# Five weight slots in place of four for the FFN input units of a decoder layer, with loads reordered and one subtraction split in time

## The reference, cut to what matters

```python
def swiglu_ffn(x, w_in, w_out):
    gate, up = jnp.split(x @ w_in, 2, axis=-1)
    return (jax.nn.silu(gate) * up) @ w_out
...
x = x + 0.5 * swiglu_ffn(rmsnorm(x, ffn1_norm[l]), ffn1_w_in[l], ffn1_w_out[l])
...
x = x + 0.5 * swiglu_ffn(rmsnorm(x, ffn2_norm[l]), ffn2_w_in[l], ffn2_w_out[l])
```

## Time and profile before

| | us |
|---|---|
| median of 3 runs | 1762.08 (1761.79 to 1765.37) |
| profiled execution, its own time | 1763.39 |
| span of the profiled execution, first to last instruction | 1761.5 |

### The profile page before, as it was taken

The page is one execution under the profiler, slowest core; times in us unless marked ns, Lnnn a source line. Parts: engine busy times, 40 slices in busy tenths (PEclk is TensorE's granted clock), DMA queues, the critical chain, the costliest instruction groups (busy, mean ns, idle before and its releaser), DMA issues.

```text
span 1761.5 us, 21397 instructions
## 1 busy us (share of the span) xinstructions
PE 1749.1 (99%) x7976; PEld 1448.9 (82%) x7976; DVE 1483.3 (84%) x1778; ACT 1108.7 (63%) x1461; POOL 95.1 (5%) x111
## 2 busy tenths in 40 slices
PE   9999999999999999999999999999999999999999
PEld 7888888888888888888888888888888888987887
DVE  7999989998999998575655655988999999899998
ACT  7666666666666666454545554666666666666665
POOL 0000010000000001100000000100000000000000
PEclk9999999999999999999999999999999999999999
DMA  9898888886655556555455457888888897764762
GB/s 378 285 287 270 263 257 262 259 254 193 248 215 193 202 214 209 189 181 185 155 186 168 168 168 269 268 261 262 265 272 273 266 278 213 241 214 165 256 214 92
DMA packets 168326, 405.02 MB, mean 230 GB/s; under 512 B 9016, under 2 KB 18000, under 8 KB 162848
## 3 DMA queue, kind: packets, MB, share of 16 engines
q1 hardware_dynamic: 154208, 342.03, 54.0%
q0 software_dynamic: 12896, 59.67, 16.7%
q10 hardware_dynamic: 1120, 1.97, 0.3%
HBM read 351.57 MB, written 5.79 MB: 203 GB/s over the span
## 4 chain that ended last, share of the span: by engine, by line
PE 94%; DVE 3%; ACT 1%; issue 1%; DMA 0%; SPq 0%; DVEq 0%; ACTq 0%
PE bank L697 8%; PE bank L669 8%; PE bank L671 8%; PE bank L670 8%; PE bank L699 8%; PE bank L698 8%; PE bank L630 7%; PE bank L632 7%; PE bank L631 6%; PE bank L777 5%; PE bank L779 5%; PE bank L778 5%; PE bank L803 3%; PE bank L805 3%; PE bank L804 3%; DVE wlo L1332 2%
## 5 line engine op out<-in xcount | busy, mean ns | idle before, releaser
L1332 DVE TENSOR_TENSOR wlo<-raw,whi 128x1024 fp32r<-128x1024 f32 (+1 forms) x506 | 609.2, 1209 | 199.1 <-ACT whi L973 187.4
L973 ACT ACTIVATE whi<-raw 128x1024 fp32r<-128x1024 f32 (+1 forms) x506 | 527.8, 1048 | 356.0 <-PE bank L632 183.8
L697 PE MATMUL bank<-whi,xs 128*128 128x512 f32 (+1 forms) x608 | 239.3, 394 | 6.4 <-DVE wlo L1332 5.5
L699 PE MATMUL bank<-whi,xs 128*128 128x512 f32 (+1 forms) x608 | 234.7, 386 | 0.0
L698 PE MATMUL bank<-wlo,xs 128*128 128x512 f32 (+1 forms) x608 | 234.3, 385 | 0.0
L973 ACT ACTIVATE whi<-tsum 128x1024 fp32r<-128x1024 f32 (+1 forms) x120 | 122.2, 1037 | 98.6 <-PE bank L699 47.0
L777 PE MATMUL bank<-whi,aw_hi 128*128 128x512 f32 x420 | 164.4, 391 | 0.0
L779 PE MATMUL bank<-whi,aw_lo 128*128 128x512 f32 x420 | 163.6, 389 | 0.0
L778 PE MATMUL bank<-wlo,aw_hi 128*128 128x512 f32 x420 | 163.5, 389 | 0.0
L630 PE MATMUL bank<-whi,xs 128*128 128x512 f32 x384 | 155.1, 404 | 0.4 <-DVE wlo L1332 0.4
L1332 DVE TENSOR_TENSOR wlo<-tsum,whi 128x1024 fp32r<-128x1024 f32 (+1 forms) x120 | 141.7, 1194 | 12.4 <-ACT whi L973 10.7
(11 more groups left out here) (225 smaller groups left out, 3092.4 us busy)
## 6 DMA issues: line engine op xcount, KB each, us to landing
raw<-ffn_w_in SPq DMA_DIRECT2D x86, 1024.0 KB, 7.0
raw<-ffn_w_out SPq DMA_DIRECT2D x84, 1024.0 KB, 6.7
raw<-w_in SPq DMA_DIRECT2D x48, 1024.0 KB, 5.0
raw<-ffn_w_in SPq DMA_DIRECT2D x75, 512.0 KB, 7.6
tsum<-raw POOLq DMA_DIRECT2D x35, 1024.0 KB, 7.0
minis<-ffn_w_in SPq DMA_DIRECT2D x72, 256.0 KB, 8.0
last_plain<-ffn_w_in SPq DMA_DIRECT2D x36, 512.0 KB, 6.0
raw<-w_out SPq DMA_DIRECT2D x16, 1024.0 KB, 4.9
```

The costliest lines, as they stand in the source:

```text
L697: mm(banks[b][:, 0:w], xs[:, k + i, 0, tok], hi, start=starts[b] and k + i == 0, stop=False, skip_group_check=True)
L699: last = mm(banks[b][:, 0:w], xs[:, k + i, 1, tok], hi, start=False, stop=k + i == last_k, skip_group_check=True)
L973: A(whi[:, h % SLOTS, 0:n_el], src, ACT.Copy).then_inc(weights_hi, 1)
L1332: V.tensor_tensor(wlo[:, h % SLOTS, 0:n_el], src, whi[:, h % SLOTS, 0:n_el].bitcast(f32), ALU.subtract).then_inc(weights_lo, 1)
```

## The change

Four things, all in the units of both FFNs:

1. In units 1 to 9 the halves go through a ring of five slots. The fifth, `fifth`, lies in slot 1 of `raw`. Slots in these units are counted from the first half of unit 1, modulo five; before and after them a half's slot is h % 4 as it was. ACT waits for the half that had the slot last, whichever it was (`RING_LAST`). At unit 1 ACT also waits until all of unit 0 has been split, since `fifth` lies where one of its pieces was.
2. Each of the four form pieces has one slot of `raw` and of `minis` of its own (2, 3, 4, 0) in place of five in turn.
3. SP's order in a unit j is B11 of the next unit; UA, UB, UC; B12, B22, B21 of the next unit; GA, GB, GC of the next unit. It was B12 of the next unit; UA, UB; B22; UC; B21; B11 of the unit after the next; GA, GB, GC.
4. The gate's first combination adds bank X first, between B22's two halves on DVE, and subtracts bank Y afterwards, ahead of T4; it was first Y ahead of T4, then X between T4's two halves. PE waits ahead of UA for the subtraction, as before.

```diff
-FORM_SLOTS, FIRST_FORM_SLOT = 5, 2
+FORM_RAW = (2, 3, 4, 0)
+FIFTH_RAW = 1
+FIRST_OUT_SLOT = 2
...
+def ring_slot(h):
+    for u in range(2):
+        if unit_half(u, 1) <= h < unit_half(u, UNITS - 1):
+            return (h - unit_half(u, 1)) % (SLOTS + 1)
+    return h % SLOTS
+
+RING_LAST, _seen = {}, {}
+for _h in range(END):
+    RING_LAST[_h] = _seen.get(ring_slot(_h), -1)
+    _seen[ring_slot(_h)] = _h
...
-            return (4 * j + i + FIRST_FORM_SLOT) % FORM_SLOTS if i < 4 else RAW_SLOTS + (i - 4) % 3
+            return FORM_RAW[i] if i < 4 else RAW_SLOTS + (i - 4) % 3
...
+        place[0] = raw_at + FIFTH_RAW * 4 * W * 4
+        fifth = sb("fifth", [P, 2, 2 * W], f32r)
...
+        def hi_of(h):
+            return whi[:, ring_slot(h), :] if ring_slot(h) < SLOTS else fifth[:, 0, :]
...
+                if slot == FIFTH_RAW:
+                    for u in range(2):
+                        if OUT_P[u] <= n < (QKV_P, END_P)[u]:
+                            sp.wait_ge(weights_used, unit_half(u, UNITS - 1))
...
                         plain_piece(u, 1, "GC")
-                        form_piece(u, 2, "B11")
                     else:
                         if j + 1 < UNITS:
-                            form_piece(u, j + 1, "B12")
-                        plain_piece(u, j, "UA")
-                        plain_piece(u, j, "UB")
+                            form_piece(u, j + 1, "B11")
+                        for name in ("UA", "UB", "UC"):
+                            plain_piece(u, j, name)
                         if j + 1 < UNITS:
-                            form_piece(u, j + 1, "B22")
-                        plain_piece(u, j, "UC")
-                        if j + 1 < UNITS:
-                            form_piece(u, j + 1, "B21")
-                            if j + 2 < UNITS:
-                                form_piece(u, j + 2, "B11")
-                            plain_piece(u, j + 1, "GA")
-                            plain_piece(u, j + 1, "GB")
-                            plain_piece(u, j + 1, "GC")
+                            for name in ("B12", "B22", "B21"):
+                                form_piece(u, j + 1, name)
+                            for name in ("GA", "GB", "GC"):
+                                plain_piece(u, j + 1, name)
...
-                pe.wait_ge(w_done, first + 1)
+                pe.wait_ge(gate_added, 2 * first + 1)
...
             def split(h, src, n_el):
-                if h >= SLOTS:
-                    act_e.wait_ge(weights_used, h - SLOTS + 1)
-                A(whi[:, h % SLOTS, 0:n_el], src, ACT.Copy).then_inc(weights_hi, 1)
+                if RING_LAST[h] >= 0:
+                    act_e.wait_ge(weights_used, RING_LAST[h] + 1)
+                A(hi_of(h)[:, 0:n_el], src, ACT.Copy).then_inc(weights_hi, 1)
...
+                if j == 1:
+                    act_e.wait_ge(weights_lo, base)
...
-                for i in range(2):
-                    split(base + B22 + i, form_half(n22, i, w), w2)
+                split(base + B22, form_half(n22, 0, w), w2)
+                dve.wait_ge(weights_used, base + GC + 1)
+                dve.wait_ge(copied, 3 * first + 1)
+                V.tensor_tensor(gset[:, s, 1, 0:w], X[:, 0:w], gset[:, s, 1, 0:w], ALU.add).then_inc(x_added, 1)
+                split(base + B22 + 1, form_half(n22, 1, w), w2)
                 plain_split("UA", UA)
                 dve.wait_ge(weights_used, base + T3_B22 + 1)
-                dve.wait_ge(copied, 3 * first + 1)
-                V.tensor_tensor(gset[:, s, 1, 0:w], gset[:, s, 1, 0:w], Y[:, 0:w], ALU.subtract).then_inc(w_done, 1)
+                dve.wait_ge(x_added, first + 1)
+                V.tensor_tensor(gset[:, s, 1, 0:w], gset[:, s, 1, 0:w], Y[:, 0:w], ALU.subtract).then_inc(gate_added, 1)
                 split(base + T4, t_half(0, w), w2)
-                dve.wait_ge(w_done, first + 1)
-                V.tensor_tensor(gset[:, s, 1, 0:w], X[:, 0:w], gset[:, s, 1, 0:w], ALU.add).then_inc(gate_added, 1)
                 split(base + T4 + 1, t_half(1, w), w2)
```

More of the change, by code:

```diff
@@ L148, in raw_slot @@
             q = OUT_LOADS[c][i] - 2 * OUT_GROUPS[c]
-            return 3 + (2 * c * OUT_GROUPS[0] + OUT_LOADS[c][i]) % 3 if q < 0 else (c * ACT_PLAIN[0] + q + FIRST_FORM_SLOT) % 3
+            return 3 + (2 * c * OUT_GROUPS[0] + OUT_LOADS[c][i]) % 3 if q < 0 else (c * ACT_PLAIN[0] + q + FIRST_OUT_SLOT) % 3
     for first, slots in ((IN_P[1], RAW_SLOTS), (QKV_P, QKV_RAW_SLOTS), (0, RAW_SLOTS)):
         if n >= first:
-            return (n - first + (sum(ACT_PLAIN) + FIRST_FORM_SLOT if slots == QKV_RAW_SLOTS else 0)) % slots
+            return (n - first + (sum(ACT_PLAIN) + FIRST_OUT_SLOT if slots == QKV_RAW_SLOTS else 0)) % slots
 def transfers(n):
@@ L304, in piece_half, with lo_of @@
             return raw[:, raw_slot(n), i * n_el:(i + 1) * n_el]
+        def hi_of(h):
+            return whi[:, ring_slot(h), :] if ring_slot(h) < SLOTS else fifth[:, 0, :]
+        def lo_of(h):
+            return wlo[:, ring_slot(h), :] if ring_slot(h) < SLOTS else fifth[:, 1, :]
         def plain_half(n, n_el):
@@ L374, in layer @@
         x_stored, x_back = sem("x_stored"), sem("x_back")
-        sums_done, t2_added, t4_added, t_summed, copied, w_done, gate_added, c11_done = (
-            sem(n) for n in ("sums_done", "t2_added", "t4_added", "t_summed", "copied", "w_done", "gate_added", "c11_done"))
+        sums_done, t2_added, t4_added, t_summed, copied, x_added, gate_added, c11_done = (
+            sem(n) for n in ("sums_done", "t2_added", "t4_added", "t_summed", "copied", "x_added", "gate_added", "c11_done"))
         sq_done, hss_ready, hms_ready, hr_ready, hsc_ready, qn_ready, qk_psum, qkT_ready, v_ready = (
@@ L573, in add_piece @@
                 pool.dma_start(tsum[:, 0:4 * w], raw[:, raw_slot(n), 0:4 * w], accum_op=ALU.add).then_inc(done, 16)
-                pool.dma_start(tmini[:, 0:w], minis[:, raw_slot(n), 0:w], accum_op=ALU.add).then_inc(done, 16)
+                pool.dma_start(tmini[:, 0:w], minis[:, FORM_RAW.index(raw_slot(n)), 0:w], accum_op=ALU.add).then_inc(done, 16)
             def x_again(u):
@@ L666, in tile @@
             def tile(h, i, bank_out, stationary, k, w, start, stop):
-                hi, lo = whi[:, h % SLOTS, i * w:(i + 1) * w], wlo[:, h % SLOTS, i * w:(i + 1) * w]
+                hi, lo = hi_of(h)[:, i * w:(i + 1) * w], lo_of(h)[:, i * w:(i + 1) * w]
                 st_hi, st_lo = stationary(k, 0), stationary(k, 1)
@@ L693, in plain @@
                         pe.wait_ge(x_ready, 2 * h + i + 1)
-                    hi, lo = whi[:, slot, i * w:(i + 1) * w], wlo[:, slot, i * w:(i + 1) * w]
+                    hi, lo = hi_of(h)[:, i * w:(i + 1) * w], lo_of(h)[:, i * w:(i + 1) * w]
                     for b in range(TB):
@@ L970, in split @@
             def split(h, src, n_el):
-                if h >= SLOTS:
-                    act_e.wait_ge(weights_used, h - SLOTS + 1)
-                A(whi[:, h % SLOTS, 0:n_el], src, ACT.Copy).then_inc(weights_hi, 1)
+                if RING_LAST[h] >= 0:
+                    act_e.wait_ge(weights_used, RING_LAST[h] + 1)
+                A(hi_of(h)[:, 0:n_el], src, ACT.Copy).then_inc(weights_hi, 1)
             def split_two(h, src0, src1, w):
-                act_e.wait_ge(weights_used, h - SLOTS + 1)
-                A(whi[:, h % SLOTS, 0:w], src0, ACT.Copy)
-                A(whi[:, h % SLOTS, w:2 * w], src1, ACT.Copy).then_inc(weights_hi, 1)
+                act_e.wait_ge(weights_used, RING_LAST[h] + 1)
+                A(hi_of(h)[:, 0:w], src0, ACT.Copy)
+                A(hi_of(h)[:, w:2 * w], src1, ACT.Copy).then_inc(weights_hi, 1)
             def mixer_split(t):
@@ L1331, in split @@
                 dve.wait_ge(weights_hi, h + 1)
-                V.tensor_tensor(wlo[:, h % SLOTS, 0:n_el], src, whi[:, h % SLOTS, 0:n_el].bitcast(f32),
+                V.tensor_tensor(lo_of(h)[:, 0:n_el], src, hi_of(h)[:, 0:n_el].bitcast(f32),
                                 ALU.subtract).then_inc(weights_lo, 1)
@@ L1336, in split_two @@
                 dve.wait_ge(weights_hi, h + 1)
-                V.tensor_tensor(wlo[:, h % SLOTS, 0:w], src0, whi[:, h % SLOTS, 0:w].bitcast(f32), ALU.subtract)
-                V.tensor_tensor(wlo[:, h % SLOTS, w:2 * w], src1, whi[:, h % SLOTS, w:2 * w].bitcast(f32),
+                V.tensor_tensor(lo_of(h)[:, 0:w], src0, hi_of(h)[:, 0:w].bitcast(f32), ALU.subtract)
+                V.tensor_tensor(lo_of(h)[:, w:2 * w], src1, hi_of(h)[:, w:2 * w].bitcast(f32),
                                 ALU.subtract).then_inc(weights_lo, 1)
```

15 lines of the change are left out of this document (7 added, 8 removed).

## The result

The changed kernel is slower: 1765.62 us (median, 1764.24 to 1767.88) against 1762.14 (1761.57 to 1765.37), a ratio of 1.0018, 95% interval [1.0012, 1.0024]. The prediction, 1757.6 us, is 8 us too low, and the result lies above its range: 3.5 us more in place of 4.5 less. The profiled execution has a span of 1764.6 us against 1761.5.

A forecast was written before the change was run, and what follows sets the result against it. PE (TensorE), busy 99% of the span, was taken to bound the kernel, so only its waiting could change. Terms -9.4 - 0.3 + 5.25 = -4.5 us, off the median 1762.08, gave 1757.6 us; range 1755.2 to 1762.3.

The forecast's parts named there:

- Ring of five, GA: Units 2 to 9 of both FFNs: PE's wait at GA goes, 0.59 us per unit, -9.4 us (-7.7 to -10.2).
- the loads: Reordered loads and a slot per form piece, in both FFNs: 0, up to 1 us per FFN in the upper bound.
- X's place: X added between B22's halves, ahead of PE's UA: nothing queues behind a wait, 0, covered by 1.5 us.
- The borders: Unit 10 of FFN 1 +2.5, unit 10 of FFN 2 +0.85, unit 1 of FFN 2 +1.9; together +5.25 us (4.5 to 6).
- B12's move: B12's load goes out when T3_B22 is split and lands before `sum_t1` needs it, with 1.8 us of cover.
- late-B12 rival: B12 shares the engines with other transfers, `sum_t1` waits in every unit; 1770 us at a 10.5 us landing; chance 0.07.
- Unit 1 of FFN 1: The fifth slot closes a 0.2 us gap between B11's halves; with hitches at the unit's end -0.3 us (0 to -0.5).
- the sentence on W_out: Before FFN-out: W_out's second load waits for B21's slot; 0, up to 1 us for each FFN in the upper bound.
- The clock: Rival: after PE's waits at three borders the clock falls to 1.2 GHz, giving back the 4.5 us; 1762 us; chance 0.04.
- unmoved GA: Rival: SwiGLU waits for something other than DVE's queue, GA's 0.48 us stay; +5, 1767 us; chance 0.05.

The follow-up runs named there:

- e5: Changed kernel with the ring of four halves of before, the new loads, slots and X's place kept; 1770.95 us, ratio 1.0048 against the kernel before.
- e7: Changed kernel with the addition of X put back behind T4's first half; 1767.33 us, ratio 1.0029 against the kernel before.
- e3: Changed kernel with the edits of e1 and e2 together; 1753.60 us, ratio 0.9949 against the kernel before.
- e2: Changed kernel with the ring of five renumbered so that halves at its borders take the slot free longest; 1760.44 us, ratio 0.9986 against the kernel before.
- e1: Changed kernel with W_out's first five transfers in slots 1, 2, 3, 4, 0 instead of 2, 0, 3, 4, 1; 1759.08 us, ratio 0.9979.
- e6: Changed kernel with POOL's 2 MB transfer of x started ten halves later; 1761.39 us, ratio 0.9994 against the kernel before.
- e8: e3 with UC's transfer issued behind B12 of unit 2, in unit 1 alone; 1752.20 us, ratio 0.9942 against the kernel before.
- e9: Changed kernel with the edits of e8 and e6 together; 1754.73 us, ratio 0.9958 against the kernel before.

## Why the prediction was wrong

**Ring of five, GA: right, the total in part by luck.** -9.7 measured for -9.4. Units 2 to 9 are at 41.03 each, and PE waits nowhere in them. But e5 gives 0.09 of a unit's gain to the loads or X's place, which were put at 0: the ring itself is worth 16 x 0.52 = 8.3 us, inside the bounds of its term, and the other 1.4 was not foreseen.

**The borders: right.** 2.61, 0.97 and 1.85 measured, together 5.43, for 2.5, 0.85 and 1.9; the waits stand at T1 (2.08) and GA (0.99), as described, and renumbering the ring took 5.2 us away. The upper bound of the sum, added up from its terms, is +0.3 and not 0; the result lies outside either.

**B12's move: right.** In unit 4 of FFN 1 it left at 200.45, its `minis` part landed at 206.91 and `sum_t1` read it at 208.62: 1.7 us of cover for 1.8. The late-B12 rival did not come. The landing of 6.1 us after the issue of that part is near the row of its new place, and not near 10.3, the longest landing, by which the rival was priced; POOL's sum beside it is over at 203.38. The Trainium skill ("DMA: Bandwidth & Descriptors", section "Queues, rings and completion order") has each DMA engine take turns between the queues that have work. Where a transfer of POOL runs beside the loads for longer, as x does at W_out's fifth, the trace is in line with that: 16.3 us with it, 11.2 without.

**X's place: 0, as far as it can be told.** By its median e7 leaves 0.1% open.

**Unit 1 of FFN 1: -0.3 predicted, +0.73 measured.** The 0.2 at T2 came in this execution (from 1.10 to 0.88 between the starts of two matmuls), but the idle time there goes from none to 0.95 in the ten profiles, from none to 0.93 with the same code (e3, e2), so that the ring gave it is not shown. The order of the loads was priced by when UA, UB and UC are used ("each has 8 us or more until its use"), and not by what they share the engines with: UC's transfer runs beside POOL's sum of B21, which T4's copy waits for, and UB starts 0.75 late.

**The failing step** is the sentence on W_out: "W_out's second load waits for B21's slot, free at T4 and not at B22; its half is split after the unit's end. 0, with up to 1 us for each FFN in the upper bound." It measured +2.67 and +3.77, 6.4 us; with -9.7, +5.4, +0.7 and the mixer's 0.1 that is the +3.0 by which the two profiled executions differ. The wait was seen, but priced for the half of that load alone. Its cost is the queue: SP issues in order, so three loads stood behind it whose slots came free sooner (in e1 the transfers into those slots left 2.2 us and more before B21's), the engines were empty for four slices, and the four left within 1.5 us. Each has time in hand by itself; together with the sixth and x they need 17.5 us at the rate of the DMA, and the fifth is needed after 12.4 (452.39 to 464.75). The rows that would have told were in the trace of before: in FFN-out 2 the fifth transfer needed 16.5 us and ACT sat 2.67 us for it, so the cover at this place was used up before the change took anything from it. The bound of 1 us for each FFN had no row behind it.

**The clock: the fall came, and cost little.** The prediction gave 0.04 to a clock that falls at the borders. The changed kernel's profile has 1.00 in each stage. In e6's, with the same wait of 2.08 us ahead of unit 10 of FFN 1, PE ran at 0.50 about a microsecond later (us, then busy us of PE, PEld, DVE, ACT, POOL, clock, DMA share, GB/s):

```profile
426.50:429.80 3.30, 3.30 (x12) 3.30 (x12) 3.30 (x6) 1.73 (x3) 1.75 (x2) 0.50 0.40 80
```

Unit 10 took 33.57 us there and 33.28 at the full clock: PE came later to GA and did not wait its 0.99. The mean granted clock of the timed runs says how common this is: 0.997 to 0.999 in 11 of the changed kernel's 20, 1.000 in the other nine and in all 38 runs of the kernel before that were timed beside the experiments. Those nine average 1765.5 us and the eleven 1766.0, so the clock is not what took the gain.

The chance of slower, 0.12, was for B12 and an unmoved GA. That the transfers are late was right in kind, at another place and for another reason.

## What to carry to other kernels

Price a wait on an in-order queue by everything that stands behind it, and then by the rate at which the bunch can be served, not by the one transfer that waits. Before a ring or a slot table is renumbered, follow the numbers over its borders, both of the ring itself and of the next stage's first transfers that inherit its slots: here a base of 1 in place of 2 and a ring that follows on turn a loss of 0.18% into a gain of 0.5%. Where an engine idles for a transfer in the trace of before, the cover at that place is zero, even if PE does not stop.

## What the runs showed of the hardware

- **The clock after a wait of PE.** A wait of 2.84 us left the granted clock at 1.00 (after); one of 2.86 at the same matmul was followed by 6.1 us at 0.50, the 1.2 GHz level (e2), and one of 2.79 by some 2.8 us of it (e5). Of the waits of 2.08 us ahead of unit 10, one was followed by 3.3 us at 0.50 (e6), the others by none (after, e1, e7). In e3, e8 and e9, where these waits are gone, all 15 runs have a mean clock of 1.000. The stage as a whole lost less than the slow stretch itself: 0.9 us in e2, 0.3 in e6. What decides whether the clock falls was not tried.
- **The transfers share some 420 GB/s.** One transfer of 1 MB takes 5.4 us to land (450.88 to 456.25, after); as the fourth of a bunch beside 2 MB of POOL's it takes 16.3. In FFN-out 1 the sum of bytes over 420 GB/s told within 1.3 us when the last one landed; in FFN-out 2, with its slower start, it would have been some 4 us too early (1542, an estimate, for 1546.40).
- **Late transfers are paid for long.** Behind the late fifth one the stage lost about 0.2 us at a time for some 80 us more. With W_out's other slots two such losses are left, as in the kernel before; in e9, without the hole but with x late, they are back. Which engine is short in each of these restarts was not followed.
